# Seven block products for half of the second MLP projection's first two column blocks, with weight sums made by accumulating DMAs

## The reference, cut to what matters

```python
def squared_relu_mlp(h, w1, w2):          # w1: 2048 x 8192, w2: 8192 x 2048
    return jnp.square(jax.nn.relu(h @ w1)) @ w2
...
x = x + squared_relu_mlp(rmsnorm(x, norm_mlp[l]), w_mlp_in[l], w_mlp_out[l])
...
mod = jax.nn.silu(c) @ w_ada + b_ada      # w_ada: 2048 x 6144, c: one row
```

## Time and profile before

| | |
|---|---|
| median of the runs | 1684.78 us |
| the profiled execution | 1684.11 us, of which the span of the program is 1682.3 us |
| busy in the span | PE 99%, DVE 66%, ACT 47%, POOL 3% |
| phase P2 | about 381 to 1087 us of the span |
| TensorE's granted clock | full, 2.4 GHz, in all of P2 |

### The profile page before, as it was taken

One profiled execution on the slowest core, in us unless ns is written; L12 is line 12 of the kernel. 1 busy time (PEld: TensorE's weight loads), 2 busy tenths in 40 slices (PEclk: granted clock), 3 DMA queues, 4 the chain that ended last, 5 costly groups with the idle time before them and its releaser, 6 DMA issues.

```text
span 1682.3 us, 25173 instructions
## 1 busy us (share of the span) xinstructions
PE 1673.5 (99%) x9397; PEld 1453.9 (86%) x9397; DVE 1112.0 (66%) x1118; ACT 795.6 (47%) x989; POOL 55.2 (3%) x61
## 2 busy tenths in 40 slices
PE   9999999999999999999999999999999999999998
PEld 7888888888888888888888888799999988888886
DVE  5454545557877677767876777775675556767754
ACT  5645664554443444334433445454444454444443
POOL 1000000000000000000000000000000001101100
PEclk9999999999999999999999999999999999999999
DMA  9643645467787788777787777675555655555562
GB/s 310 220 133 110 189 138 175 163 211 269 255 280 251 260 278 277 253 232 279 266 289 243 254 260 256 214 235 168 174 164 177 196 190 188 182 192 174 196 205 88
DMA packets 171692, 361.48 MB, mean 215 GB/s; under 512 B 11008, under 2 KB 17472, under 8 KB 171344
## 3 DMA queue, kind: packets, MB, share of 16 engines
q1 hardware_dynamic: 169392, 352.37, 63.3%
q0 software_dynamic: 2064, 7.56, 1.2%
q10 hardware_dynamic: 144, 0.26, 0.0%
HBM read 358.00 MB, written 2.15 MB: 214 GB/s over the span
## 4 chain that ended last, share of the span: by engine, by line
PE 97%; DVE 1%; issue 1%; DMA 0%; ACT 0%; SPq 0%; POOLq 0%; POOL 0%; ACTq 0%; DVEq 0%
PE G L762 31%; PE S L762 13%; PE S L776 12%; PE G L776 12%; PE G L745 10%; PE G L779 6%; PE S L779 6%; PE S L715 1%; PE G L751 1%; PE S L1147 0%; DMA raw<-in_w_in 0%; DVE window_sums L1830 0%; PE S L1140 0%; PE S L1126 0%; PE S L1014 0%
## 5 line engine op out<-in xcount | busy, mean ns | idle before, releaser
L1453 DVE TENSOR_TENSOR w_lo<-raw,w_hi 128x1024 fp32r<-128x1024 f32 (+1 forms) x573 | 704.1, 1245 | 416.5 <-ACT w_hi L1181 415.0
L1181 ACT ACTIVATE w_hi<-raw 128x1024 fp32r<-128x1024 f32 (+1 forms) x574 | 591.6, 1046 | 593.1 <-PE G L762 176.7
L762 PE MATMUL G<-w_hi,X_pair 128*128 128x512 f32 (+2 forms) x1456 | 444.5, 383 | 0.1
L762 PEld LDWEIGHTS G<-w_hi,X_pair 128*128 128x128 f32 x1456 | 269.6, 188 | 55.4 <-issue 3.3
L762 PE MATMUL G<-w_lo,X_pair 128*128 128x512 f32 (+2 forms) x728 | 276.8, 380 | 0.0
L776 PE MATMUL S<-Y_pair,w_hi 128*128 128x512 f32 x768 | 267.0, 390 | 0.0
L776 PE MATMUL G<-Y_pair,w_hi 128*128 128x512 f32 x768 | 266.8, 390 | 0.0
L779 PE MATMUL G<-Y_pair,w_lo 128*128 128x256 f32 x768 | 216.6, 282 | 0.0
L779 PE MATMUL S<-Y_pair,w_lo 128*128 128x256 f32 x768 | 216.6, 282 | 0.0
L745 PE MATMUL G<-Y_pair,w_hi 128*128 128x256 f32 x1088 | 194.0, 280 | 1.1 <-DVE Y_pair L1569 0.9
L776 PEld LDWEIGHTS S<-Y_pair,w_hi 128*128 128x128 f32 x768 | 144.2, 188 | 30.2
(11 more groups left out here) (346 smaller groups left out, 1406.2 us busy)
## 6 DMA issues: line engine op xcount, KB each, us to landing
raw<-in_w_in SPq DMA_DIRECT2D x142, 512.0 KB, 4.5
raw<-in_w_mlp_in SPq DMA_DIRECT2D x128, 512.0 KB, 5.3
raw<-in_w_mlp_out SPq DMA_DIRECT2D x128, 512.0 KB, 6.5
ada_w<-in_w_ada SPq DMA_DIRECT2D x64, 768.0 KB, 4.7
raw<-in_w_out SPq DMA_DIRECT2D x64, 512.0 KB, 4.4
raw<-in_w_merge SPq DMA_DIRECT2D x64, 512.0 KB, 4.2
raw<-in_w_branch_attn SPq DMA_DIRECT2D x16, 512.0 KB, 4.4
raw<-in_w_branch_pool SPq DMA_DIRECT2D x16, 512.0 KB, 6.0
```

The lines of the kernel that those rows point to most:

```text
L762: ins = nc.tensor.matmul(token_bank(bank, tt)[:, 0:n], a[:, c0 + c, tok], w[:, s % SPLIT, c, 0:n], start=first and c == 0 and k == 0, stop ...
L1181: nc.scalar.activation(w_hi[:, s % SPLIT, :, 0:n], raw[:, k, :, 0:n], ACT.Copy).then_inc(hi_ready, 1)
L1453: nc.vector.tensor_tensor(w_lo[:, s % SPLIT, :, 0:n], raw[:, k, :, 0:n], w_hi[:, s % SPLIT, :, 0:n], ALU.subtract).then_inc(lo_ready, 1)
```

## The change

In each quarter the down projection is reordered. For the column blocks 0 and 1, the 16 chunks of hidden features are taken in two sets of 8 chunks (4 row blocks of 256, k = 0 to 3). In each set, k = 2, 3 are done as before (4 ordinary subs, N0A to N1B). For k = 0, 1 the 2 x 2 x 2 block product (token half, k, column block) is done with seven products instead of eight, V1 to V7 (Winograd's form of Strassen's scheme), each a sub of 6 matmuls. V1, V2 and V3 use weight tiles as loaded; V5, V6, V7 and V4 need sums and differences of weight tiles. ACT makes the negative of a tile (`neg`, 8 per quarter, 128 x 1024 each), and a DMA issued by POOL then adds a tile of `w_mlp_out` to it on its way from HBM (`add_to`, `accum_op=ADD`, 512 KB, 8 per quarter). The sums hang together: `neg2` starts from the sum t1 (V5's weights), `neg4` from t2 (V6's). The activation sums are made by DVE (`sum_x`, `sum_lo`) and ACT (`sum_hi`). The results (seven products, and the ordinary subs on top of three of these and in one more bank) fill all eight PSUM banks through both sets and are combined on DVE at the end (`mixB` to `mixG`; `mixA` on ACT). Column blocks 2 and 3 follow as before.

A quarter has 70 subs in place of 64: 32 up, 2 x 11, 16 down. SP makes 62 weight loads per quarter. The rectifier and the square move from one DVE operation to two ACT operations. 28 of the 32 ada operations of a quarter move into slots 0 to 31 and 4 to slots 56 to 59, because `ada_w`'s memory holds weight sums in between; loads 14 and 15 wait for this. SP's loop over the quarters is written out. At 2 places of a quarter one of the 4 conversion slots is skipped.

```diff
-SPLIT_AT = 60
+SPLIT_AT = 66
+ADA_OPS = [0, 1, 2, 3, 4, 5, 6, 7, 10, 11, 12, 13, 14, 15, 16, 17, 18, 19, 20, 21, 22, 23, 26, 27, 28, 29, 30, 31,
+           56, 57, 58, 59]
+ADA_LOADS = [0, 2, 13, 15, 17, 19, 23, 25, 27, 29, 31, 33, 35, 39, 53, 54]
+ADA_EARLY = 14
+UP = 4 * len(ALL)
+SETS, SET_SUBS = 2, 11
+MIXED = SETS * SET_SUBS
+MLP_SUBS = UP + MIXED + 2 * len(ALL)
+SKIPS_AT = (13, 21)
+V1, N1A, V3, N1B, V2, V5, N0A, V6, V7, N0B, V4 = range(SET_SUBS)
+SET_FROM = {V1: 0, N1A: 1, V3: 3, N1B: 2, V2: 6, N0A: 4, V7: 5, N0B: 7}
+NEGATED = [(26, 0, 1), (28, 0, 3), (30, 0, 2), (33, 0, 4), (35, 1, 1), (38, 1, 3), (39, 1, 2), (44, 1, 4)]
...
+            def load_mlp(r, i, w, row0, col):
+                at2, k = PHASE["P2"][0], r % RAW
+                if r < UP + RAW:
+                    freed = r - RAW
+                elif r < UP + 3 * RAW:
+                    g = (r - UP) // RAW - 1
+                    freed = UP + SET_SUBS * g + SLOT_SPLIT[k]
+                    if k in (0, 3):
+                        sp.wait_ge(act_side, done("A", f"neg{3 if k else 1}_{g}", i))
+                else:
+                    freed = r - RAW + MLP_SUBS - MLP_LOADS
+                sp.wait_ge(lo_ready, count(at2 + freed, (i, MLP_SUBS), 1))
...
+            def mixed(s, loop, i, j):
+                g, k = divmod(j, SET_SUBS)
+                if k == V1:
+                    pe.wait_ge(dve_side, done("D", f"hlo{2 * g}", i))
+                if k == N1A:
+                    pe.wait_ge(dve_side, done("D", f"hlo{2 * g + 1}", i))
+                if k == V3:
+                    pe.wait_ge(dve_side, done("D", f"sum_lo{g}", i))
+                pe.wait_ge(lo_ready, count(s, loop, 1))
...
+                if k in SET_SUMS:
+                    act.wait_ge({V5: t1_in, V6: t2_in, V7: t3_in, V4: t4_in}[k], loop[0] * 32 + 16 * (g + 1))
...
+                elif name[:3] == "neg":
...
+                    elif k == 2:
+                        act.wait_ge(t1_in, i * 32 + 16 * (g + 1))
+                        from_ = w_added(g, 1)
...
+                    else:
+                        act.wait_ge(t2_in, i * 32 + 16 * (g + 1))
+                        from_ = w_added(g, 2)
...
+                    nc.scalar.activation(w_added(g, k), from_, ACT.Copy, scale=-1.0).then_inc(act_side, 1)
...
                 elif name[:3] == "hid":
                     b = int(name[3:])
                     act.wait_ge(dve_side, done("D", f"up{b}", i))
+                    nc.scalar.activation(right[:, :, :], right[:, :, :], ACT.Relu).then_inc(act_side, 1)
+                    act.wait_ge(act_side, step("A", name, 1, i))
+                    nc.scalar.activation(chunked(hid), right[:, :, :], ACT.Square).then_inc(act_side, 1)
+                    act.wait_ge(act_side, step("A", name, 2, i))
                     nc.scalar.activation(x_hi[:, 4 * b:4 * b + 4, :], chunked(hid), ACT.Copy).then_inc(act_side, 1)
...
+            def add_to(g, k, i):
+                pool.wait_ge(act_side, done("A", f"neg{k}_{g}", i))
+                p, n = ADDED_AT[k]
+                row0 = i * D_MODEL + P * SUB * (4 * g + p)
+                pool.dma_start(w_added(g, k), t["w_mlp_out"][row0:row0 + P * SUB, NW * n:NW * (n + 1)]
+                               .rearrange("(c p) n -> p c n", p=P), accum_op=ALU.add
+                               ).then_inc({1: t1_in, 2: t2_in, 3: t3_in, 4: t4_in}[k], 16)
```

More of the change, by code:

```diff
@@ L252 @@
         stage("P1", _s + 2, f"out_sq{_n}", A=2)
[L253 to L261, removed]
+stage("P2", 3, "mlp_rms", D=3)
+for _s in range(UP + SET_SUBS + V6):
+    for _g in range(SETS):
+        if _s == 16 * _g + 9:
+            stage("P2", _s, f"sum_x{_g}", D=4)
+        if _s == 16 * _g + 10:
+            stage("P2", _s, f"sum_hi{_g}", A=1)
+        if _s == 16 * _g + 11:
+            stage("P2", _s, f"sum_lo{_g}", D=1)
+    for _j in range(4):
+        if _s == 8 * _j + 7:
+            stage("P2", _s, f"up{_j}", A=1, D=1)
+        if _s == 8 * _j + 8:
+            stage("P2", _s, f"hid{_j}", A=3)
+        if _s == 8 * _j + 9:
+            stage("P2", _s, f"hlo{_j}", D=1)
+    if _s == UP + SET_SUBS + V1:
+        stage("P2", _s, "mixA", A=1)
+    for _at, _g, _k in NEGATED:
+        if _s == _at:
+            stage("P2", _s, f"neg{_k}_{_g}", A=1)
+    if _s == UP + SET_SUBS + N1B:
+        stage("P2", _s, "mixB", D=2)
+_set = UP + SET_SUBS
+stage("P2", _set + V6, "mixC", D=2)
+stage("P2", _set + V7, "mixD", D=2)
+stage("P2", _set + V4, "mixE", D=2)
+stage("P2", UP + MIXED, "mixF", D=2)
+stage("P2", UP + MIXED + 1, "mixG", D=2)
+stage("P2", 61, "ada_fold0", D=2)
+stage("P2", 62, "ada_fold1", D=2)
+stage("P2", 63, "down2", D=2)
 stage("P2", SPLIT_AT, "down3_0", P=1, D=1)
@@ L1177, in main @@
                     return
-                act.wait_ge(raw_in[k], v if loop is None else loop[0] * (16 * loop[1] // RAW) + v)
+                r = raw_of(s, loop)
+                g, k = set_sub(s, loop)
+                if k in SET_SUMS:
+                    act.wait_ge({V5: t1_in, V6: t2_in, V7: t3_in, V4: t4_in}[k], loop[0] * 32 + 16 * (g + 1))
+                else:
+                    act.wait_ge(raw_in[r % RAW], raw_count(r, loop))
                 if s >= SPLIT:
-                    act.wait_ge(used, count(s, loop, 1 - SPLIT))
-                nc.scalar.activation(w_hi[:, s % SPLIT, :, 0:n], raw[:, k, :, 0:n], ACT.Copy).then_inc(hi_ready, 1)
+                    here = s - PHASE["P2"][0]
+                    early = in_mlp(loop) and any(k <= here < k + SPLIT - 1 for k in SKIPS_AT)
+                    act.wait_ge(used, count(s, loop, 1 - (SPLIT - 1 if early else SPLIT)))
+                nc.scalar.activation(w_hi[:, split_of(s, loop), :, 0:n], source(s, loop)[:, :, 0:n], ACT.Copy).then_inc(hi_ready, 1)
             def halves(name, dst, chunks, i=None, gain=None):
@@ L1425, in norm_sums @@
                     else:
-                        act.wait_ge(dve_side, step("D", f"down{n}", tt + 1, last) if n < 3 else step("D", f"down3_{tt}", 1, last))
+                        act.wait_ge(dve_side, done("D", "mixG", last) if n < 2 else step("D", "down2", tt + 1, last) if n < 3
+                                    else step("D", f"down3_{tt}", 1, last))
                     src = x_nf[:, tt, :] if k else x[:, tt, NW * n:NW * (n + 1)]
@@ L1903, in norm_sums @@
                     dve.wait_ge(norm_f_in, 16)
[L1904 removed]
                 for tt in (range(NT) if n < 3 else (int(name[-1]),)):
[L1906 removed]
+                    dve.wait_ge(dve_side, done("D", "mixG", last) if n < 2 else step("D", "down2", tt + 1, last) if n < 3
+                                else step("D", f"down3_{tt}", 1, last))
                     if n:
```

263 lines of the change are left out of this document (219 added, 44 removed).

## The result

The changed kernel takes 1770.3 us (median of 4 runs, 1765.4 to 1771.6) against 1684.8: a ratio of 1.0503 with a 95% interval of 1.0482 to 1.0524. The forecast was 1678 in a range from 1673 to 1703, so the change went the other way and ended outside the range.

A forecast was written before the change was run, and what follows sets the result against it. PE, busy 99%, was taken to bound the kernel. Saved matmuls -10.9, border waits +2.6, transfer waits 4 x 0.4 sum to -6.7 us, from 1684.11 to 1677.4; stated as 1678, range 1673 to 1703.

The forecast's parts named there:

- What is removed: Down projection on PE: 90 matmuls per set in place of 96, 48 fewer in all, saving 10.9 us.
- I take the same rate: PE in the sets: operands keep their shapes, so each matmul still takes 0.2267 us.
- I take 6, cost 0: Up projection: ada loads land in 6 us and DVE catches up 0.7 us per slot, so nothing is lost.
- my own threshold: Up projection: from an ada load landing of 6.4 us on, DVE's lateness grows.
- Rival 1: Up projection: ada loads land in about 8 us, DVE waits, PE starves; 12 us in all, 1689; chance 0.09.
- DVE 88% full, no bound: Up projection: DVE's work over 16 slots is 39.3 us of 44.4, so DVE does not bind.
- The ACT timetable at the border: Up projection to set 0: ACT's added operations make PE wait 0.65 us per quarter at V5, 2.6 in all.
- L = 7.8: Accumulating transfers: 7.8 us from a neg's end to the sum's landing, costing 0.4 us per quarter.
- the tightest mark: Set 1, neg1 to neg2: L up to 7.4 us costs nothing; each us beyond costs PE one per quarter.
- Rival 3: Accumulating transfers slow, ACT standing at neg2 and neg4, kernel slower; chance 0.12 for L 9.1 to 10.6, 0.09 beyond.
- its middle case: Accumulating transfers landing in 9.1 to 10.6 us: 1685 to 1703, chance 0.12.
- Its doubled transfer: Accumulating 512 KB counts as two transfers, L 11.8 us: 11.7 us per quarter, 47 in all, 1721; chance 0.09.

The follow-up runs named there:

- the last kernel: The change with halved ada loads, no general wait before negatives, later negative places, the square on DVE, and plain copies instead of accumulating transfers: 1682.0 us, ratio 0.9987.
- the cut kernel: The changed kernel with 4 of 16 ada loads per quarter and no accumulating transfers: 1706.0 us; also without the general wait before neg and sum_hi: 1684.4 us.

## Why the prediction was wrong, step by step

**What is removed: right in count, at best 0.6 of its size.** A quarter's two sets were to take 40.8 us against 43.5. Some rows of the chain of the last kernel (start, us, count), where almost nothing waits, give the true figure:

```profile
471.38 5.50 PE S L927 x24
...
486.09 1.40 PE S L927 x6
...
506.60 1.36 PE S L927 x6
...
513.40 43.52 PE G L906 x192
```

From 471.38 to 513.40 are 42.0 us: 1.5 saved in this quarter, not 2.7, and by PE's starts 1.5, 1.0 and 0.8 in the others, 4.8 in all. The 1.2 in between divide so, by the starts: 0.6 are two waits of about 0.3, before N1B and V5 of set 0 (0.65 was predicted, at V5); 0.45 is lost in the subs right behind them, whose matmuls start up to 0.33 apart at first; the rest is "I take the same rate": in set 0 V3, V6 and V7 take 1.40 us for their six matmuls. In set 1 every sub keeps 0.2267 us per matmul. And PE loses 2.5 us, 1.9 of them in one wait (the row of L904 above stands in this kernel too), near the end of the last quarter, for a conversion whose chain runs through the last ada operation and both folds; the four ada operations moved to slots 56 to 59 and the folds behind them were costed at nothing there. So even without trouble the gain is about 2 us (1682.0 measured), at the limit of what can be told from nothing, and not 6.7.

**"I take 6, cost 0": the step that failed most, 45 us of the 86.** The ada loads land in 7.3 us, and my own threshold stood at 6.4. My 6 came from a median of 4.7 where a load had more room around it; the longest landing of the same row, 8.6, was as near as my value. Rival 1 had this mechanism and a landing of about 8. It was given 0.09 and priced at 12 us, since I let DVE catch up and let 2 us be spare. Neither holds: ACT's `hid` waits for DVE's `up` add, so DVE's lateness goes back to ACT's conversions and stops DVE once more, up to 3.2 us at a block's end, and the lateness is carried into set 0. There the last ada load, which the prediction had not set beside the sums, lands in up to 11.2 us. "DVE 88% full, no bound" was right as a count (the operations measured 0.42 where I took 0.4) and useless as a test: the order of arrival binds, not the sum.

**The ACT timetable at the border: 0.65 us predicted, 22 us missed.** With all else out of the way PE waits 0.63 us before V2 and 0.55 before V5, where one wait of 0.65 before V5 was predicted. So the timetable was short by half for the waits I gave it, which is under 1 us a quarter. It did not have the general wait, which was in the unchanged part of `stage` and only became dear when stages with no need of DVE were put between ACT's conversions.

**L = 7.8: too small, and 18 us where 1.6 were taken.** From issue all 32 sums land in 9.2 at the median, and L is 0.3 more; only the 24 in `w_sum`, with 7.3, look like the forecast. And it is the one late link that counts: t1 of set 1, the tightest mark (7.4), took L = 9.4 to 10.5 in the four quarters, with `neg3`'s sum in flight beside it. That sums overlap was not in the estimate of L. What the accumulate adds to a copy, 1.5 us as estimated, is 3.3 by the medians of all 32 (9.2 against 5.9). Rival 3 said where ACT would stand, and its middle case (L of 9.1 to 10.6, up to 7 us a quarter) had the size: 18 us measured with halved loads. Its doubled transfer (11.8, 47 us) was reached by the overlapping sums of set 0 alone. (A slip beside this: by the prediction's own marks the matmuls' saving is used up from L = 8.9 on, not 9.1.) The Trainium skill, Collectives: The Full Stack, section "The bandwidth ceiling: the fold count and why AG ≠ RS ≠ AR", has a reduce at half the rate of a copy for its two source reads. Here the accumulate costs time too, but about 1.4 to 1.6 times the landing of a plain copy at the median (9.2 against 5.9 us, and 9.5 against 6.7 with the later places), not twice, and no run tells its read from its addition.

**Not in the sum at all: the clock.** The prediction had all matmuls at the full rate. After waits of several us at the border the granted clock was at its lower level for part of the time, 41 us in all, which cost about 15. It went with the waits: in the cut kernel without the general wait nothing of it is left in this phase. With the ada loads away it is 14 us, with the transfers away 17, with both 14, so a part that is taken away alone takes most of it along, one more reason why 56 + 26 are not 64.

The causes in order, each taken away behind the last: general wait 1770.3 to 1748.2, halved ada loads to 1703.5, other places of the negatives to 1697.9 (1696.7 with the square on DVE), plain copies from there to 1682.0. The 88 us are thereby accounted for, in this order of taking away; in another order the shares differ, as 56 against 45 us for the ada loads shows. Not tried: sums prepared a set ahead, which would need more buffers, or placed so that no two are in flight together. Open is why the sums that overlap take so long, and why the matmuls of set 0 start a little further apart than those of set 1.

## What to carry to other kernels

When work is moved into a denser stretch, don't test the engine's sum of busy time but each load's lead: the time from "buffer free" to "needed", against the landing in that density; below it, split the load before anything else. A helper's general wait ("all earlier stages done") is free while stages are rare, and must be priced again whenever a stage is put among the conversions. And a saving of 0.6% on an engine that is busy 99% has no room for a single new wait: count what each mark can bear from the longest landing in the rows, not from the median, and look which transfers will be in flight together: here a median of 7.3 us hid landings of 10 to 14.

## What was not expected of the hardware

- An accumulating DMA of 512 KB into SBUF lands in 9.2 to 9.5 us at the median where a plain one at the same places takes 5.9 to 6.7. Some of the accumulating ones land in 6.1 us, but two that are in flight together took 9.1 to 14.5 us each, and stretched an ada load beside them from about 6 to as much as 11. The issue of an accumulating one occupies POOL 1.20 us where the plain one takes 0.72:

```profile
L2277 POOL DMA_DIRECT2D w_sum<-in_w_mlp_out x24: 1194/1203/1277, 461.0 to 1034.3; - x24
...
L2277 POOL DMA_DIRECT2D w_sum<-in_w_mlp_out x24: 722/722/756, 460.9 to 1021.4; - x24
```

- Waits of 3 to 7 us, in a phase that is otherwise solid matmuls, were followed by stretches at 1.2 GHz that cost about 15 us more, on 66 of added idle time; in the kernel whose waits were 0.5 to 1.1 us there were none.
